# Decode rows in fixed slots of every expert, and loads and gathers in another order, in a hybrid layer with routed experts

## The reference

```python
h  = x + concat(attn, ssm) @ w_out
t  = rms_norm(h, norm2)
g_idx = top1(softmax(t @ w_grp + b_grp))            # one of 4 groups
e_top, e_idx = top2(softmax((t @ w_exp + b_exp)[g_idx]))   # two of its 8 experts
gate = g_top * e_top / sum(e_top)
hid = silu(t @ w_gate[e]) * (t @ w_up[e])           # 1024 -> 128, for each chosen expert
y   = h + sum(gate_e * (hid_e @ w_down[e]))         # 128 -> 1024
```

## Time and profile before

| | |
|---|---|
| runs before, median (lowest to highest) | 812.96 us (812.08 to 813.54) |
| profiled execution | 815.63 us |
| its span, first to last instruction | 813.6 us |
| PE busy | 737.7 us, 91% |
| PEld busy | 533.9 us, 66% |
| DVE busy | 460.4 us, 57% |
| POOL busy | 302.5 us, 37% |
| ACT busy | 273.5 us, 34% |
| mean granted TensorE clock | 0.968 of full |

### The profile page before, as it was taken

One profiled execution on the slowest core, in us unless ns is written; L12 is line 12 of the kernel. 1 busy time (PEld: TensorE's weight loads), 2 busy tenths in 40 slices (PEclk: granted clock), 3 DMA queues, 4 the chain that ended last, 5 costly groups with the idle time before them and its releaser, 6 DMA issues.

```text
span 813.6 us, 13104 instructions
## 1 busy us (share of the span) xinstructions
PE 737.7 (91%) x4344; PEld 533.9 (66%) x4344; DVE 460.4 (57%) x1219; ACT 273.5 (34%) x654; POOL 302.5 (37%) x365
## 2 busy tenths in 40 slices
PE   5999999999999999999959999993998888888894
PEld 2968585867777786945535553562877767767773
DVE  1679789797979797978524774655222222222221
ACT  1453544545354555355312331211222212212221
POOL 0243343423234334322000331002476566566564
PEclk9999999999999999999979999985899999999998
DMA  9900303030302901033774887112689888888842
GB/s 313 342 27 4 104 1 106 1 106 0 105 0 63 279 7 52 0 116 104 225 248 157 302 262 263 43 52 63 198 292 290 266 281 281 265 286 277 267 100 35
DMA packets 63451, 125.77 MB, mean 155 GB/s; under 512 B 20756, under 2 KB 33076, under 8 KB 63260
## 3 DMA queue, kind: packets, MB, share of 16 engines
q1 hardware_dynamic: 47252, 99.86, 36.4%
q0 software_dynamic: 13824, 16.97, 9.1%
q10 hardware_dynamic: 2336, 8.46, 2.6%
HBM read 109.83 MB, written 49.90 MB: 196 GB/s over the span
## 4 chain that ended last, share of the span: by engine, by line
issue 21%; DMA 21%; PE 19%; DVE 17%; POOL 7%; DVEq 5%; POOLq 5%; SPq 2%; ACT 2%; ACTq 0%
DMA cum_rows<-t_dram,idx_in 9%; DMA tT<-t_dram,idx_in 8%; DVE cv L1040 7%; PE bank L1732 7%; PE bank L2058 4%; PE bank L1665 3%; POOLq L1529 2%; POOL rstd L1486 2%; PE bank L2064 2%; POOLq L1485 2%; DVEq L899 2%; POOL cv L1530 2%; DMA x<-t_dram,idx_in 2%; PE bank L1756 1%; DVEq L1038 1%
## 5 line engine op out<-in xcount | busy, mean ns | idle before, releaser
L1732 PE MATMUL bank<-w_out_sb,mix_back 128*128 128x512 f32 x256 | 121.0, 617 | 8.6 <-DMA x<-in_x_prompt 8.6
L2058 PEld LDWEIGHTS bank<-w_arena 128*128 128x128 f32 x992 | 118.2, 195 | 15.6 <-issue 14.3
L2058 PE MATMUL bank<-w_arena 128*128 128x128 f32 x992 | 118.4, 279 | 0.9 <-ACT w_arena L831 0.9
L1732 PEld LDWEIGHTS bank<-w_out_sb,mix_back 128*128 128x128 f32 x256 | 47.8, 196 | 61.5 <-issue 52.5
L1484 POOL TENSOR_TENSOR stat<-stat,eps 128x1 f32<-128x1 f32 (+4 forms) x35 | 9.5, 273 | 176.5 <-ACT junk L656 103.3
L1674 PE MATMUL bank<-w_arena,tT 128*128 128x512 f32 (+1 forms) x192 | 73.3, 537 | 1.6 <-DVE tT L1024 1.6
L1674 PE MATMUL bank<-w_arena,xT 128*128 128x512 f32 (+1 forms) x192 | 71.6, 526 | 0.0
L1040 DVE SCALAR_TENSOR_TENSOR cv<-raw,par,cv 128x128 f32<-128x128 f32 x192 | 68.7, 419 | 2.4
L1427 DVE TENSOR_TENSOR w_arena<-w_arena,bank 128x128 f32<-128x128 f32 x32 | 9.2, 288 | 103.2 <-ACT w_arena L836 103.2
L2064 PE MATMUL bank<-w_arena 128*128 128x512 f32 x124 | 58.9, 597 | 0.7 <-DVE w_arena L1427 0.7
L1714 PEld LDWEIGHTS bank<-xT,w_arena 128*128 128x128 f32 x512 | 58.4, 192 | 0.5
(11 more groups left out here) (322 smaller groups left out, 1249.0 us busy)
## 6 DMA issues: line engine op xcount, KB each, us to landing
w_arena<-in_w_gate SPq DMA_DIRECT2D x31, 512.0 KB, 5.1
w_arena<-in_w_up SPq DMA_DIRECT2D x31, 512.0 KB, 7.3
w_arena<-in_w_down SPq DMA_DIRECT2D x31, 512.0 KB, 14.9
x<-in_x_prompt SPq DMA_DIRECT2D x16, 512.0 KB, 5.5
w_arena<-in_w_in SPq DMA_DIRECT2D x3, 2048.0 KB, 14.2
mix_back<-in_x_prompt_by_channel SPq DMA_DIRECT2D x8, 512.0 KB, 3.9
cum_rows<-cum_dram SPq DMA_DIRECT2D x8, 512.0 KB, 4.6
mix_dram<-mix SPq DMA_DIRECT2D x8, 512.0 KB, 5.2
```

The source lines that it names most:

```text
L1732: ins = pe.matmul(bank[out_bank(i, c)][:, :], mix_back[tile % 2][:, k, :], w_out[:, k, 512 * c:512 * c + 512], start=k == 0, stop=k == KC - 1)
L2058: ins = pe.matmul(out[:, a * P:(a + 1) * P], gu[:, a, k, :], xgT[w % 2][:, k, :], start=k == 0, stop=k == KC - 1)
```

## The change

Expert slots. The 8 decode rows hold slots 120 to 127 of every expert and are not ranked; 120 slots remain for prompt rows (`ROWS`), and the overflow limits follow. A decode row's gate is zero in experts that it did not choose. The index list for `y_sample` and the second scatter are gone. In their place VectorE adds, expert by expert, partitions 96 to 127 of the result tile into a buffer (`decoded`, which SP has filled from `y_sample` ahead of the experts), and SP stores its last 8 rows at the end.

Gathers. In POOL's step for expert j the gather of expert j+4 stands first, and waits only until TensorE has turned buffer j; before, it stood behind both scatters of j.

Loads. The third tile's back load stands between the third and fourth state load.

Behind the last tile. ACT and VectorE copy a half of the turned rows each; ACT's square is ahead of its store; the group mask has one instruction where it had three; the gates and the value products stand ahead of the rank, which is read from PSUM without a copy; the slot table is one instruction where it was four; the router's matmuls of the last tile stand ahead of four choice matmuls; POOL's other waits stand ahead of the one for the slots.

The diff, cut:

```diff
-ROWS = P
-OVER_TILES = CHOICES // (ROWS + 1)
+ROWS = P - DEC
+OVER_TILES = 2 * SEQ // (ROWS + 1)
...
             for b in range(DEC):
+                if b == 3:
+                    load_next_back(2)
                 sp.dma_start(st_h[:, b], ...).then_inc(state_in, 16)
...
             sp.dma_start(st_raw, I["x_sample"].rearrange("b s d -> (b s) d")).then_inc(late_in, 16)
-            load_next_back(2)
             load_first(0)
...
+            sp.dma_start(decoded[ROWS:P, :], y_sample).then_inc(dec_in, 16)
...
+            sp.wait_ge(E_["dec"], NE)
+            sp.dma_start(y_sample, decoded[ROWS:P, :]).then_inc(dec_in, 16)
+            sp.wait_ge(dec_in, 32)
...
-            act_residual(act, 8)
-            act_turned_t(act, 8, P)
+            act_square(act, 8)
+            act_turned_half(act, 8)
+            act_store_h(act, 8)
...
-            dve.tensor_scalar(gmask[0:n, 0, :], con[0:n, C_IOTA:C_IOTA + NG], fi[0:n, 0:1], None, ALU.is_equal)
-            dve.drain()
-            dve.tensor_scalar(gmask[0:n, 1, :], gmask[0:n, 0, :], 1.0, BIG, ALU.subtract, ALU.mult)
-            dve.tensor_tensor(le[0:n, :, :], ..., ALU.mult)
-            dve.drain()
-            dve.tensor_tensor(le[0:n, :, :], le[0:n, :, :], ..., ALU.add)
+            dve.tensor_scalar(gmask[0:n, 0, :], con[0:n, C_IOTA:C_IOTA + NG], fi[0:n, 0:1], 1.0, ALU.is_equal, ALU.subtract)
+            dve.drain()
+            dve.scalar_tensor_tensor(out=le[0:n, :, :], in0=gmask[...], scalar=BIG, in1=lg[...], op0=ALU.mult, op1=ALU.add)
...
             dve_residual(dve, 8, 1)
             dve_ranked(7)
+            dve_turned_t(dve, 8)
             dve_choices(slice(EARLY - 4, EARLY - 2), ...)
             dve_norm2(dve, 8)
             dve_routed(8)
-            dve_ranked(8)
-            dve_choices(slice(EARLY - 2, EARLY), ...)
+            dve_gates(dve, 8, P, slot_of(8))
+            dve_values(slice(EARLY - 2, EARLY), chosen[:, EARLY - 2:EARLY])
+            dve_rank(dve, 8, P, slot_of(8))
+            dve_select(slice(EARLY - 2, EARLY), row_sel[1][:, EARLY // 2 - 2:, :])
...
-            dve.tensor_scalar(slot_f[:, 0, :], bank[1][:, 0:NE], float(EMPTY), None, ALU.add)
-            dve.tensor_copy(gate_tab[:, 0:NE], bank[1][:, NE:2 * NE])
-            slot_table(0, NE).then_inc(T["slots"], 1)
+            dve.tensor_scalar(slot_tab[:, 0:NE], bank[1][:, 0:NE], con[:, C_SLOT:C_SLOT + 1], None, ALU.add)
+            dve.tensor_copy(gate_tab[:, 0:NE], bank[1][:, NE:2 * NE]).then_inc(T["slots"], 1)
...
+            def dve_decoded(j, w):
+                dve.wait_ge(E_["ya"], j + 2)
+                dve.wait_ge(E_["yd"], j + 2)
+                dve.tensor_tensor(decoded[DEC_AT:P, :], decoded[DEC_AT:P, :], yo[w][DEC_AT:P, :], ALU.add).then_inc(E_["dec"], 1)
...
                 if more:
                     dve_turned(j + 1, (w + 1) % RING)
+                if stored is not None or w > 0:
+                    dve_decoded(j - 1, (w - 1) % RING)
...
-                if left <= NE - RING:
-                    pool.wait_ge(e_out[w], 32 * group)
+                pool.wait_ge(E_["idx"], j + 2)
+                if left > RING:
+                    pool.wait_ge(E_["turn"], j + 1)
+                    pool.sem_inc(E_["free"], 1)
+                    gather(xg[w], idx_in[w], e_x[w])
+                pool.wait_ge(T["slots"], 2)
+                if 1 < left < NE or left == NE and w == RING - 1:
+                    pool.wait_ge(e_out[(w + 1) % RING], 16 * (group + (w + 1) // RING))
                 pool.wait_ge(E_["ya"], j + 2)
                 pool.wait_ge(E_["yd"], j + 2)
-                pool.wait_ge(E_["idx"], j + 2)
...
                 scatter(yo[w], w, e_out[w])
-                if left > RING:
-                    gather(xg[w], idx_in[w], e_x[w])
...
             pe_turned(7)
-            pe_ranked(6)
             pe_out(pe, 7, 0, rear)
...
             pe_turned(8)
+            pe.wait_ge(T["lastT"], 1)
+            pe_routed(8)
             pe.wait_ge(T["part"], 4)
             pe_choices(range(EARLY - 4, EARLY - 2), early, pairs, start=False, stop=False)
-            pe_routed(8)
             pe_ranked(8)
```

More of the change, by code:

```diff
@@ L295, in layer_kernel @@
         idx_out = [sb(f"idx_out{w}", [P, 1], I32) for w in range(RING)]
-        idx_row = [sb(f"idx_row{w}", [P, 1], I32) for w in range(RING)]
         gate_col = [sb(f"gate_col{w}", [P, 1]) for w in range(RING)]
         loaded = sem("loaded")
+        dec_in = sem("dec_in")
         S = {}
@@ L305, in layer_kernel @@
         T = {}
-        for name in "init aneg q kT att cv dt xz scT bcT bc bx hup ch hst norm ssmT cnt part slots et over".split():
+        for name in "lastT init aneg q kT att cv dt xz scT bcT bc bx hup ch hst norm ssmT cnt part slots et over".split():
             T[name] = sem("m_" + name)
         E_ = {}
-        for name in ("turn xa xd up sil hid dn ya yd idx").split():
+        for name in ("turn xa xd up sil hid dn ready ya yd dec idx free").split():
             E_[name] = sem("e_" + name)
@@ L346, in layer_kernel, with ranked @@
         ORDER = (*range(TILES - 2), TILES, TILES - 2, TILES - 1)
+        def ranked(i):
+            return i - (i > ORDER.index(TILES))
         def width(tile):
@@ L942, in dve_norm2, with dve_turned_t @@
                                      op0=ALU.mult, op1=ALU.mult).then_inc(S["td"], 1)
+        def dve_turned_t(dve, i):
+            now(dve, "ttm", i)
+            last(dve, "lgm", i)
+            dve.tensor_copy(tT[:, 4:8, :], bank[6][:, :].rearrange("p (k n) -> p k n", k=4)).then_inc(T["lastT"], 1)
         def dve_router(dve, tile, n, slot):
@@ L979, in dve_router, with dve_gates @@
             dve.drain()
-            last(dve, "rankm", tile)
+            if n < P:
+                return
+            last(dve, "rankm", ranked(tile))
             dve.tensor_tensor(both[0:n, :], slot("onehot", n)[:, 0], slot("onehot", n)[:, 1], ALU.add).then_inc(S["rsel"], 1)
-        def dve_rank_read(dve, tile, n):
-            now(dve, "rankm", tile)
-            dve.tensor_copy(rankc[0:n, :], bank[7][0:n, 0:NE]).then_inc(S["rankd"], 1)
-        def dve_rank(dve, tile, n, slot):
+        def dve_gates(dve, tile, n, slot):
             now(dve, "gex", tile)
@@ L1063, in _ @@
             dve.tensor_copy(mask[:, 1, :], con[:, C_BAND + P:C_BAND + 2 * P])
+            dve.tensor_copy(rank[:, TILES], con[:, C_RANK:C_RANK + 2])
             dve_keys(0)
@@ L1612, in pool_expert @@
                 if left > RING + 1:
-                    ins = fetch_index(idx_in[(w + 1) % RING], expert(w + 1, group + 1), 0)
+                    ins = fetch_index(idx_in[(w + 1) % RING], expert(w + 1, group + 1))
                 if left > 1:
@@ L1753, in pe_router @@
             now(pe, "tt", tile)
-            last(pe, "rankd", tile)
+            last(pe, "rankd", ranked(tile))
             for k in range(KC):
@@ L1759, in pe_rank @@
         def pe_rank(pe, tile, n):
-            now(pe, "rsel", tile)
+            now(pe, "rsel", ranked(tile))
             pe.matmul(bank[7][0:n, 0:NE], strict[0:n, 0:n], both[0:n, :], start=True, stop=False)
```

127 lines of the change are left out of this document (71 added, 56 removed).

## The result

The changed kernel takes 802.73 us (median of 4 runs, 801.49 to 803.92), the kernel before 812.52 (4 runs, 810.75 to 813.54). The ratio is 0.989, with a 95% interval of 0.987 to 0.991. The change is faster, as forecast, but by 9.8 us where 20.7 were forecast, and 802.73 lies just over the range of 779 to 802. The profiled execution took 801.49 us with a span of 799.6, 14.0 less than before.

A forecast was written before the change was run, and what follows sets the result against it. TensorE was taken as nearly always busy, standing still at three places, with half the DMA engines full in the expert stage. Terms 10.1 + 0.4 + 2.9 + 5.7 + 1.6 = 20.7 us gave 792 us, range 779 to 802.

The forecast's parts named there:

- Third tile: Wait for x rows near 410 us: moving the load earlier gains 8.5 us plus 1.6 of clock, 10.1 together.
- The second rival: Third tile's gain is given back because tile 3's rows or the state come late: 800 us; 14%.
- The decode ranks: Routing: decode rows no longer get ranks, dropping four tiny matmuls and a few VectorE steps: 0.4 us.
- Behind the last tile: Shorter string of small steps before the first expert: 2.9 us, up to 1.9 more if router matmuls got higher clock.
- Expert stage: Rounds of 7.61 us: 2.5 from the removed scatter and 3.2 from the earlier gather, 5.7 us less.
- the reading: Expert stage: half of the DMA engines full all the time, the other half busy for 71%.
- the gather a round ahead: Expert stage: adds no capacity but shifts one gather and one scatter out of the full engines' time: 3.2 us.
- Each round loses one scatter ... So 0.1 us a round: Expert stage: packet time of the removed y_sample scatter, bounds 0 to 0.2 a round; 2.5 us over 25 rounds.
- the signs named for being right: Among them: rounds of 7.4 to 7.6 us, waits partly for weights, gathers landing in over 14 us.
- The end: After the last expert: no second scatter to y_sample, gaining 1.6 us (0.8 to 1.85).
- The first: Rival: engines not full, wait a closed loop; the earlier gather removes all 27.3 us: 771 us; 12%.
- The third: Rival: GpSimd waits each round for the scatter three rounds back, deciding from 20.3 us landing; slower, 828 at 24; 4%.

The follow-up runs named there:

- e11: Kernel before with only the third tile's load moved ahead of the fourth state load: 802.83 us, 0.990.
- e4: Kernel before with the gather first in GpSimd's step and the wait for the scatter three rounds back, both scatters kept: 807.92 us, 0.995.
- e2: Changed kernel with another slot table that spreads an expert's ranks over both halves of the partitions: 768.24 us, 0.947.
- e3: Kernel before with a slot table that puts every second block of ranks in partitions 64 to 127: 787.49 us, 0.970.
- e8: Changed kernel with a finer table than e2: rows dealt out singly, partitions 88 to 95 filled last: 761.17 us, 0.939.
- e1: Changed kernel with the gather put back behind the scatter, as before the change: 801.99 us, 0.988.
- e5: Kernel before without the scatter to y_sample in every round, all else kept: 814.47 us, 1.005.
- e6: Changed kernel plus, behind each scatter, an empty one with all 128 indices out of bounds: 791.9 us, 0.976.
- e9: Changed kernel plus two empty scatters behind each real one: 805.19 us, 0.994.
- e14: Changed kernel plus an empty scatter of 64 rows from partitions 64 to 127 behind each real one: 802.8 us, 0.990.
- e13: Changed kernel plus an empty scatter of 64 rows from partitions 0 to 63 behind each real one: 803.38 us, 0.991.
- e7: Changed kernel with slots 120 to 127 empty, so decode rows are never gathered: 802.77 us, 0.990.
- e15: Changed kernel plus two 128x512 products on GpSimd behind each scatter, no packets and no drain: 804.17 us, 0.991.
- e10: Changed kernel plus two drains and two 128x256 additions on GpSimd behind each scatter, no packets: 882.89 us, 1.089.

## Why the prediction was wrong

**Third tile: right.** 10.1 forecast; from 417.42 to 408.49 and from 5.28 to 3.60 are 8.9 + 1.7 = 10.6, and e11 alone gives 8.1 in the medians (810.9 to 802.83). The second rival is out.

**Up to the last tile: half seen.** The decode ranks give the 0.4 forecast. By the last tile's transposes (544.22 before, 529.17 now) the kernel is 15.05 ahead; 0.7 of the rest are shorter waits for VectorE, and 3.2 are two slow stretches of the kernel before, behind 495 and 533 us, that the changed kernel does not have. Such stretches come and go from kernel to kernel (none there in e4, two in e11), so I do not count them to the change. With one profile of each kernel, whether they also come and go between executions is not shown.

**Behind the last tile: mechanism right, size low.** 2.9 forecast, 21.72 - 17.11 = 4.6 measured. From the choice (`both`) to the gather's issue it is 4.97 us instead of 7.11, the 2.1 that were worked out; the router's matmuls take 1.98 instead of 3.58 at the higher clock, which the prediction had set down as a bound. Copying the two halves at once gave 1.0 (547.13 - 544.22 before, 531.12 - 529.17 now) where 0.5 were forecast. The mask gave its 0.3 (552.95 - 552.04 before, 535.00 - 534.42 now), but a later cast starts 0.35 us late (536.02 - 535.34, before 553.62 - 553.29), for a reason that the rows do not show; so from the router's matmuls to the choice it is 3.6 us in both.

**Expert stage: the failed step.** 5.7 us less were forecast, 7.0 more came, and these 12.7 are more than the whole miss. Half of the reading was right: where the rows lie sets the stage (e2, e3, e8), as it would if eight engines were full, and rounds are not set by the gather's length. Of the two terms the gather a round ahead gave 4 us in the kernel before (e4), where 3.2 were forecast, but nothing in the changed kernel (e1: 801.99 without it, 802.73 with it). The sentence that failed is "Each round loses one scatter ... So 0.1 us a round", with a bound of "0 to 0.2". With its 2.5 us, and 1.85 at the end, leaving out that scatter alone should have gained 4.4; e5 lost 3.1 (811.4 to 814.47). The packets were priced by the time they take, and not by what they do to the order in which rows and weights are served. Their time was priced well: GpSimd's queue holds the engines for 3.5% per MB with the empty packets (31.5% for 9.03 MB in e6) and without them (29.5% for 8.37). And the signs named for being right did not come: rounds from 7.4 to 7.6, gathers that land in over 14 us. What the removal costs depends on the kernel: the stage got 3.2 us longer in e5, and an empty scatter put back makes it 10.7 shorter in e6. How the 7.0 split into the removal and the rest of the change is not shown. The held the clue: 6,798 packets of rows against 6,888 of weights, a ratio of 0.99. The ratio of the two queues' packets from 620 to 740 us, with what TensorE waits for:

| kernel | row packets / weight packets | waits for, longest us | us |
|---|---|---|---|
| e9 | 1.33 | gathers, 3.0 | 805.2 |
| before | 0.99 | gathers, 1.3 | 812.5 |
| e4 | 1.00 | weights, 1.4 | 807.9 |
| e6 | 1.02 | weights, 0.9 | 791.9 |
| e14 | 0.83 | weights, 2.9 | 802.8 |
| e13 | 0.82 | weights, 2.7 | 803.4 |
| e1 | 0.67 | weights, 3.6 | 802.0 |
| e7 | 0.66 | weights, 3.8 | 802.8 |
| after | 0.65 | weights, 4.2 | 802.7 |
| e5 | 0.63 | weights, 3.9 | 814.5 |
| e15 | 0.63 | weights, 3.4 | 804.2 |

With as many packets in both queues, rows land about as late as the weights do (21.6 and 22.5 us in e6, 14.1 and 14.9 before). In the kernels below 0.9 the rows are through in 8 to 11 us whichever way they are issued, and the weights take over 21. (e9's time is set by GpSimd, as said above.) A picture that fits, and is not shown packet by packet: while TensorE runs at 6.24 a round, the rows take their full time first and the weights fall behind; then TensorE stops, no rows are issued, and the weights catch up. That the queues take turns is inferred from these landings and ratios. What is shown is the cause one step up: taking the second scatter out makes the lumps (e5), as many empty packets put back end them (e6), half as many do not (e13, e14), and GpSimd's time alone does not (e15). The Trainium skill's page "DMA: Bandwidth & Descriptors" (section "Queues, rings and completion order") states that an engine goes round between the queues that have work, a packet of several descriptors at a time. The landings agree with turns, though no run shows that a packet of the trace, here at most a row of 4 KB, is that unit; e13 and e14, which have as many transfers as e6 but fewer packets, speak against one turn for each transfer. In e8 the ratio is 0.77 and nothing waits, so the ratio matters only where the rows crowd one half of the partitions.

The stage of e6, in the columns used above:

```profile
546.22:770.71 224.49, 204.44 (x1360) 164.96 (x1361) 88.06 (x120) 48.74 (x92) 140.36 (x177) 0.98 0.82 260
```

What the lumps cost against e6 is 235.2 - 224.5 = 10.7 us: 5.9 of idle time of TensorE (26.0 against 20.1) and 4.8 of longer matmuls (209.2 against 204.4 us busy). That the same engine share brought 4% less of weights is in part the rows' larger share (29.5% against 28.4%), in part a longer time for a packet of weights (56.2% of 16 x 120 us over 6,602 is 163 ns, before 159). Why a packet takes longer in the lumps stays open.

**The end: right.** 1.6 forecast, 19.4 - 18.1 = 1.4.

**Rivals.** The first gave 771 for engines that are not full; steady rounds of 6.24 exist, but only when the rows are spread. The third, a loop over GpSimd's wait for scatters, is not in the changed kernel, where GpSimd waits for no scatter. It is there in e4, but the scatters land in 19.6 us, just under the 20.3 from which it was to decide. The actual rival, an even flow that breaks up, was not on the list.

## What to carry to other kernels

Before removing a transfer that moves nothing, count the packets of every queue beside it: it may be what holds two queues in step, and its removal is then worth what the new order of service is worth. Ask which partitions carry a gather's valid rows; a table that deals them over all partitions was worth some 41 us here (802.73 to 761.17). And an even wait of 1.3 us a round is cheaper than the same sum in lumps, because TensorE came out of the five longest waits here at the lower clock: it idled 2.2 us less than before, and its matmuls took 9.2 us longer. Not every such wait does it: in e1 the 32 matmuls behind a wait of 3.25 us took 3.81.

## What was not expected of the hardware

- An indirect transfer in every round whose 128 indices are all out of bounds made a kernel some 11 us faster (802.7 to 791.9).
- Two drains on GpSimd behind an indirect transfer held it 5.4 us (e10); without drains, some 2 us of GpSimd's work in every round cost no time that can be measured (e15, 0.991 against 0.989).
- Issuing an empty scatter takes GpSimd 1.54 us, hardly less than one with rows (1.59).
- TensorE runs for some us at the lower clock (8 matmuls in 5.3 to 5.4 us instead of 3.7; before, the granted clock is 0.69 from 533.34 to 538.70 us) without a long wait ahead, twice in some kernels and never in others.
